# Five instead of four ordinary gate and up pairs at the head of each feed-forward stage, with VectorE's work in another order

## The reference

```
x = x + 1/2 * SwiGLU_1(RMSNorm(x))        # SwiGLU: (silu(x @ w_gate) * (x @ w_up)) @ w_down, D_FF 2816
h = RMSNorm(x);  P = h @ W_in
y_a = ConformerConv(P_glu);  y_b = Mamba2SSD(P_z, P_xBC, P_dt)
x = x + (sigmoid(g_a) * y_a + sigmoid(g_b) * y_b) @ W_out
x = x + 1/2 * SwiGLU_2(RMSNorm(x))
y = RMSNorm(x)
```

## Time and profile before

| | |
|---|---|
| median of 3 runs | 1884.74 us (1882.38 to 1888.89) |
| the profiled execution | 1883.59 us, its span 1881.8 us |
| TensorE busy | 1789.4 us, 95% of the span |
| VectorE busy | 1331.1 us, 71% |
| ScalarE busy | 853.0 us, 45% |
| mean granted TensorE clock | 0.967 |

### The profile page before, as it was taken

One profiled execution on the slowest core, in us unless ns is written; L12 is line 12 of the kernel. 1 busy time (PEld: TensorE's weight loads), 2 busy tenths in 40 slices (PEclk: granted clock), 3 DMA queues, 4 the chain that ended last, 5 costly groups with the idle time before them and its releaser, 6 DMA issues.

```text
span 1881.8 us, 29519 instructions
## 1 busy us (share of the span) xinstructions
PE 1789.4 (95%) x11927; PEld 1742.4 (93%) x11927; DVE 1331.1 (71%) x1958; ACT 853.0 (45%) x1504; POOL 94.8 (5%) x149
## 2 busy tenths in 40 slices
PE   7799999998899999999999999998999799999996
PEld 7799999998889899989889998998999799999995
DVE  6863873774648888989899899765556854863754
ACT  5441441343567438636853763255234432541432
POOL 0000000000011011020101101010000000000000
PEclk9899999999889899899999989999999899999998
DMA  4112212213143244143425413231222112212212
GB/s 157 75 68 90 90 68 90 90 66 137 42 124 103 62 152 136 45 146 126 116 65 155 130 50 116 79 131 66 70 79 79 68 68 91 90 68 90 90 47 77
DMA packets 49431, 173.60 MB, mean 92 GB/s; under 512 B 6768, under 2 KB 6928, under 8 KB 44688
## 3 DMA queue, kind: packets, MB, share of 16 engines
q1 hardware_dynamic: 38736, 137.41, 21.2%
q0 software_dynamic: 10560, 34.31, 6.4%
HBM read 155.49 MB, written 16.20 MB: 91 GB/s over the span
## 4 chain that ended last, share of the span: by engine, by line
PE 84%; DVE 7%; ACT 5%; issue 3%; DMA 1%; DVEq 0%; ACTq 0%; SPq 0%; POOLq 0%
PE ps L1564 52%; PE ps L1625 23%; PE ps L1582 3%; PE ps L1760 2%; PE ps L1771 1%; DVE v L1287 1%; DVE w_lo L942 1%; PE ps L1754 1%; PE ps L1741 1%; PE ps L1748 1%; PE ps L1591 1%; ACT w_hi L510 1%; DVE t_lo L1078 1%; ACT acb L778 1%; DVE pair L1311 0%
## 5 line engine op out<-in xcount | busy, mean ns | idle before, releaser
L1564 PE MATMUL ps<-xa_hi,w_hi 128*128 128x320 f32 x1440 | 348.5, 324 | 7.1 <-DVE w_lo L942 7.0
L1625 PE MATMUL ps<-t_hi,w_hi 128*128 128x320 f32 x1008 | 314.5, 312 | 25.3 <-issue 25.1
L1564 PE MATMUL ps<-xa_lo,w_hi 128*128 128x320 f32 x1440 | 332.7, 313 | 0.0
L1564 PE MATMUL ps<-xa_hi,w_lo 128*128 128x320 f32 x1440 | 332.4, 312 | 0.0
L1625 PE MATMUL ps<-t_lo,w_hi 128*128 128x320 f32 x1008 | 313.6, 311 | 0.0
L1625 PE MATMUL ps<-t_hi,w_lo 128*128 128x320 f32 x1008 | 313.6, 311 | 0.0
L510 ACT CAST w_hi<-w_raw 128x1024 fp32r<-128x1024 f32 (+2 forms) x184 | 175.3, 953 | 264.8 <-PE ps L1564 227.7
L1564 PEld LDWEIGHTS ps<-xa_hi,w_hi 128*128 128x128 f32 x1440 | 246.2, 192 | 23.2 <-issue 12.7
L942 DVE TENSOR_TENSOR w_lo<-w_raw,w_hi 128x1024 fp32r<-128x1024 f32 (+2 forms) x184 | 203.2, 1105 | 85.4 <-ACT w_hi L510 83.5
L1564 PEld LDWEIGHTS ps<-xa_lo,w_hi 128*128 128x128 f32 x1440 | 245.3, 191 | 0.0
L1564 PEld LDWEIGHTS ps<-xa_hi,w_lo 128*128 128x128 f32 x1440 | 245.0, 191 | 0.0
(11 more groups left out here) (248 smaller groups left out, 2811.8 us busy)
## 6 DMA issues: line engine op xcount, KB each, us to landing
w_raw<-in_w_mix SPq DMA_DIRECT2D x56, 512.0 KB, 3.3
raw_b<-in_w_sp SPq DMA_DIRECT2D x18, 1024.0 KB, 4.8
w_raw<-in_w_sp SPq DMA_DIRECT2D x18, 1024.0 KB, 4.8
w_raw<-in_w_down SPq DMA_DIRECT2D x32, 512.0 KB, 3.3
w_raw<-in_w_tail SPq DMA_DIRECT2D x32, 512.0 KB, 3.3
acb<-cum_dram POOLq DMA_DIRECT2D x20, 512.0 KB, 6.7
w_raw<-in_w_gu SPq DMA_DIRECT2D x16, 512.0 KB, 3.5
w_raw<-in_w_ssm SPq DMA_DIRECT2D x32, 256.0 KB, 2.6
```

What stands on the lines that cost most here:

```text
L1564: last = nc.tensor.matmul(psj[:, b, u, 0:TH], w[:, cols], act_in[:, k, u * TH:(u + 1) * TH], start=(k == 0 and n == 0), stop=(k == chunks ...
L1625: last = nc.tensor.matmul(ps[:, sp_set(n) + BANK[q], 0:TH], w[:, k * P:(k + 1) * P], t[:, X_OF[q], k * TH:(k + 1) * TH], start=(first and ...
```

## The change

`ORD` becomes 5: each stage has five ordinary pairs and then runs of 3, 8 and 6 seven-product pairs (17 instead of 18). In detail:

- A fifth gate and up job per stage, with its loads, splits, gate, silu, up, hidden, high and low; one seven-product pair less.
- The hidden blocks move: 0 and 1 into `hid_early`, over the place of the seventh sum's high part (`t_hi[:, X_22]`), 2 into `acc`, 3 and 4 both into `hid`. So `t_high(X_22)` now waits for `h_low` of the first two, and `sum_sp` no longer waits for any.
- VectorE's order before the first seven-product pair is new: `gate(3)` and the splits of the fifth pair come early, `up(3)` and `hidden(3)` before most of the weight work, and the `h_low`s after `gate(4)`.
- ScalarE's order follows it.

More of the change, by code:

```diff
@@ L129, in build @@
         raw_b = sb("raw_b", [P, 4, KH * P])
-        s_at = place[0]
         w_sum = sb("w_sum", [P, 4, KH * P])
-        hid_buf = at(s_at, "hid_buf", [P, 3, T])
+        hid_early = at(t_at - KH * TH * 4, "hid_early", [P, 2, T])
         gate_s, up_s = sq[:, 0], sq[:, 1]
         silu_g, hid = pair[:, 1], pair[:, 0]
+        hid_of = [hid_early[:, 0], hid_early[:, 1], acc[:], hid, hid]
         mix_c, mix_d, c12 = sq[:, 0], sq[:, 1], acc[:, 0:TH]
@@ L1055, in hidden @@
                     dve.wait_ge(silu_ready, ORD * f + i + 1)
-                    nc.vector.tensor_tensor(hid_buf[:, i] if i < ORD - 1 else hid, silu_g, up_s,
+                    nc.vector.tensor_tensor(hid_of[i], silu_g, up_s,
                                             ALU.mult).then_inc(hid_ready, 1)
@@ L1110, in ffn @@
                 t_low(X_11)
-                n0 = NSP * f
-                low_sp(n0, W_A11)
+                gate(3)
+                split_lo(half + 4, 0)
                 t_low(X_T3)
                 t_low(X_T1)
-                for i in range(ORD - 1):
-                    h_low(i, hid_buf[:, i], i)
-                gate(3)
+                n0 = NSP * f
                 sum_sp(n0, W_S31)
+                up(3)
+                hidden(3)
+                split_lo(half + 4, 1)
+                low_sp(n0, W_A11)
                 sum_sp(n0, W_S2)
+                sum_sp(n0, W_S4)
                 low_sp(n0, W_S31)
                 t_low(X_T2)
+                gate(4)
[3 more added lines that the diff above has]
+                t_low(X_21)
                 low_sp(n0, W_S2)
[L1123 to L1126, removed]
+                up(4)
+                hidden(4)
+                t_low(X_22)
                 low_sp(n0, W_A)
-                h_low(3, hid, 3)
-                t_low(X_21)
+                h_low(4, hid_of[4], 4)
                 low_sp(n0, W_S4)
-                t_low(X_22)
                 half += ORD
```

## The result

The changed kernel takes 1866.2 us (median of 4 runs, 1865.9 to 1866.9) against 1883.56 us of the kernel before (1880.9 to 1888.9); the ratio is 0.9905 with a 95% interval of 0.9882 to 0.9927. It is faster, by 17.4 us; 11.6 were forecast. The time lies at the lower edge of the predicted 1866 to 1879.5 and outside the forecast's own 1870 to 1877. The profiled execution took 1866.88 us, its span 1865.1.

The account below looks back on a forecast made before the run. VectorE was taken to bound the stretch before the seven-product pairs, TensorE the rest. Per stage, 62.97 us became 14.1 + 4.0 + 37.05 + 2.0 = 57.15; gaining 11.6 in all gave 1873.1 us, range 1866 to 1879.5.

Parts of the forecast that it names:

- the forecast's own 1870 to 1877: Whole kernel: gain 10 to 12.2 us by the clock's bounds, with 1 us error per stop; forecast given 72%.
- The stop: TensorE before the seven-product pairs, waiting for VectorE's `up(4)`: 4.0 us instead of 10.8, from 83.5 to 87.5.
- the wait for ScalarE: VectorE after `gate(4)` stands 1.5 us until ScalarE's first high part of hidden blocks, at 80.1.
- The matmuls and the clock: Three seven-product pairs behind TensorE's stop: 37.05 us of matmuls plus 2.0 lost to the lower clock, per stage.
- the two bounds: Clock loss behind TensorE's stop, per stage: 1.7 us from a 3.93 us stop, 2.8 us as in the kernel before.
- The load: SyncE's `raw_b` load, expected by 69.6; rival: landing 9.4 us late shifts VectorE's list, 3.6 us lost per stage, 1892; 4%.
- The mixing instruction: VectorE, first seven-product pair: runs 96.2 to 97.0, before TensorE's seventh product wants it at 98.1 to 100.1; no stop.
- The rule on VectorE's spacing: VectorE's instructions before `up(4)` each take their whole duration: `up(4)` some 1.7 us later, gain 8 us instead of 12.
- The step that failed: Sum over both stages: 5.8 us gained in each, the second showing the same stop, 11.6 in all.
- my rivals: VectorE not late (9%, 1863); VectorE later (12%, 1876 to 1879); `raw_b` late (4%, 1892); no net change (3%, 1882).

Follow-up runs that it names:

- its copy with the small matmuls: The changed kernel with six small fp32 matmuls added at the head of TensorE's list; 1866.49 us.
- two experiments: Changed kernel with `up(4)` right behind the low parts of hidden blocks, 1865.92 us; changed kernel without TensorE's fifth-pair wait before the first seven-product pair, 1861.41 us.
- before with the small matmuls: The kernel before with six small fp32 matmuls added at the head of TensorE's list; 1879.89 us.
- the new order with four pairs: Four ordinary pairs as in the kernel before, with the changed kernel's buffers and VectorE's and ScalarE's new order; 1878.3 us.
- without the wait: Changed kernel without TensorE's wait for the fifth pair's gate and up ahead of a run's first seven-product pair using PSUM banks 4 to 7; 1861.41 us.
- the mixing moved: Changed kernel without that fifth-pair wait, and VectorE's first-pair mixing placed before the second pair's last weight sum and low part S31; 1859.34 us.
- the earlier `up(4)`: Changed kernel with `up(4)` moved ahead of two low parts of sums and one of weights; 1865.92 us.
- the later `up(4)`: Changed kernel with `up(4)` and `hidden(4)` moved behind one low part of a sum and one of weights; 1871.77 us.

## Why the prediction was right and wrong

**The stop: right.** VectorE's list was forecast instruction by instruction. `gate(4)` was to end at 78.65 and ended at 78.36; the wait for ScalarE was put at 1.5 us and was 1.48; `up(4)` near 86.45 came at 86.19, TensorE at 87.22 instead of 87.5. The whole trace stands about 0.2 us earlier than the first, which is most of the difference. The stop of 4.0 us was 3.8 and 3.9.

**The matmuls and the clock: right.** Behind the stop TensorE took 126.51 - 87.22 = 39.29 us for the three pairs and 39.39 in the second stage; 37.05 + 2.0 were forecast. The loss by the clock was 2.2 to 2.3, in the middle between the two bounds. It isn't fixed: in three further traces, two of this kernel and one of its copy with the small matmuls, the same stops cost 1.5 to 2.6. This accounts for the stages' gain of 5.65 and 5.45 us against 5.8.

**The load: the rival that came near.** `raw_b` landed at 68.2 and VectorE wanted it at 69.2. The margin of 1 us is the thinnest in the stretch. The prediction added two loads' times one after the other (3.8 and 5.5 us) and so expected 69.6. But the 5.5 of before already stood for a load with one of 512 KB issued 0.4 us ahead of it, as after; the first load of the fifth pair had landed at 57.0. By the 19 cases without a fetch (5.3 to 5.5 us) it would have landed near 66. The 2.3 us more go with the fetch, which the prediction didn't have: that 69.6 and 68.2 are close is luck.

**The mixing instruction: right in its cover.** Put at 96.2 to 97.0, it started at 97.30, since VectorE stood 1.25 us for a high part of weights of the second pair; TensorE had no stop there. Without the first stop it is the next one in line, as two experiments showed.

**The rule on VectorE's spacing** would have put `up(4)` at about 88.2; it came at 86.19, and the small spacing of the earlier trace rows is in the rows after as well (1.47 from 79.84 to 81.31 for two). The sum by the rows was right. In the Trainium skill, "VectorE: DVE Perf Modes", the section on the DRAIN that the prediction cites also says that a next instruction that is not held starts earlier; the prediction left that out, and the rows agree with it.

**The step that failed** is the sum's "5.8 per stage; the second stage shows the same stop, so 11.6 in all". It takes the rest of the program as unchanged in time because it is unchanged in its instructions. The stages gave 11.1 us; 5.6 more came from the stretches between and behind them. Of these 3.0 are the mixer's first group: 4.5 for a stop of 3.42 us that I took for a fixed cost and the low clock behind it, less 1.5 lost at the group's end. The stop is a collision of a store with a fetch of TensorE's instructions, and an ordinary pair for a seven-product pair puts 12 matmuls and 12 weight loads more ahead of it in TensorE's list. None of my rivals had a term outside the stages, though TensorE's wait at that line was in the very list that I read (14.8 us, longest 3.9; after, 11.7). Against before with that collision taken away (1879.89), the changed kernel (1867.38, same set) gains 12.5 us, close to the 11.6; the stages' share of it in the traces of these two is 11.0.

**What stays open.** 2.2 us come from the token sums at the end of both stages, which the low clock covers before and not after. The end of stage one took 11.4 to 11.5 us in all three traces of before and of before with the small matmuls, and 10.4 in all four of the changed kernel, with and without them (11.0 in the one of the new order with four pairs). So it goes with the program too, but no run here shows what in the program decides it. Nor do I know why one trace without the wait had the fetch at +1.34 us and one with the same list on TensorE, and the mixing moved, at -0.54, or why in the mixer's fourth group it came at +1.42 with the earlier `up(4)` and at -0.9 to -1.9 with the same list in the changed kernel. The length of TensorE's list moves the fetch, but doesn't fix its place alone.

## What to carry to other kernels

When an engine that isn't the bottleneck overall holds up the one that is in one stretch, more work for the bottleneck there can be the remedy: 1.8 us of added matmuls bought 6.9 us of stop. Price such a change by walking the late engine's list with start-to-start times, and then ask which wait is next: here the weights, then the mixing instruction. And before the gain of a change is put down to it, cut both traces at the same landmarks: what moved where nothing was edited is not the change's mechanism, and may be a collision that a few more instructions would also have moved.

## What the runs showed of the hardware

Instruction fetches share the DMA engines with the kernel's data. A 16 KB fetch that began 1.3 to 1.6 us after the issue of a 256 KB store put its landing from 2.3 us to 5.3 to 6.7 us, in 5 of 5 such stores and none of 47 others, and VectorE waited 2.1 to 3.5 us for it. A fetch just behind the issue of a 1 MB load put it from 5.3 to 5.5 us to 6.0 to 7.9. The number of instructions on TensorE's list moves the fetch: 12 small matmuls and 12 loads in a wait at the start of the kernel moved it by 1.5 to 2.8 us against the store, and made before 3.2 us faster. The kernel before, with the collision, also spreads more, 1878.1 to 1890.8 us, against 1877.8 to 1881.7 with the small matmuls and 1865.6 to 1868.6 for the changed kernel in the 13 runs of it and of its copy with them. A spread needs no collision, though: with the later `up(4)` the 7 runs go from 1865.8 to 1873.3, and its one trace has none.

A stop of 3.8 to 3.9 us of TensorE cost 1.5 to 2.6 us behind it in the eight stretches of the changed kernel's three traces and the one of its copy with the small matmuls.
